# A two-layer hybrid backbone step: expert chunks in two halves over nine slots, single ada chunks, a two-expert first part

## The reference, cut to what matters

```python
def trunk_layer(x, mod, l, P, ctx):
    sh1, sc1, g1, sh2, sc2, g2 = split(mod)                # mod = silu(c) @ ada_w[l] + ada_b[l]
    h = rmsnorm(x, P['norm1_g']) * (1 + sc1) + sh1
    x = x + g1 * mixer_block(h)                            # attention, Mamba-2 scan, mLSTM, gated and merged
    h = rmsnorm(x, P['norm2_g']) * (1 + sc2) + sh2
    return x + g2 * expert_choice_ffn(h, ...)

def ssd_scan(...):                                         # per chunk of 128 tokens, both directions
    decay = exp(where(causal, seg, -inf))                  # seg = acum_i - acum_j
    y_diag = einsum('bcihn,bcjhn->bcijh', Cc, Bc) * decay * dt_j  @ xc

def expert_choice_ffn(h, router_w, w_gate, w_up, w_down):  # 16 experts; each takes its best tokens
    aff = softmax(xt @ router_w);  g, idx = top_k(aff.T, cap)        # cap = 16 context, 32 latent
    xe = xt[idx]
    hid = silu(xe @ w_gate) * (xe @ w_up)                  # 1024 x 1024 each
    out.at[idx].add((hid @ w_down) * g)
```

## Time and profile before

| | us |
|---|---|
| median of 3 runs (lowest, highest) | 2168.41 (2166.9, 2176.54) |
| the profiled execution's own time | 2157.21 |
| its span | 2155.4 |
| PE busy | 1932.9 (90%) |
| DVE busy | 632.4 (29%) |
| ACT busy | 419.7 (19%) |
| DMA | 546.5 MB, mean 254 GB/s |

### The profile page before, as it was taken

One profiled execution on the slowest core, in us unless ns is written; L12 is line 12 of the kernel. 1 busy time (PEld: TensorE's weight loads), 2 busy tenths in 40 slices (PEclk: granted clock), 3 DMA queues, 4 the chain that ended last, 5 costly groups with the idle time before them and its releaser, 6 DMA issues. The chain is left out here.

```text
span 2155.4 us, 21845 instructions
## 1 busy us (share of the span) xinstructions
PE 1932.9 (90%) x8320; PEld 1000.1 (46%) x8320; DVE 632.4 (29%) x1640; ACT 419.7 (19%) x957; POOL 38.4 (2%) x67
## 2 busy tenths in 40 slices
PE   6998989999988898988999899899988898989887
PEld 3554645555544433343354455554555334343433
DVE  1223335434241213121022242453443222131202
ACT  2122312222111111111121223212221111111112
POOL 0000000000000000000000000000000000000000
PEclk9999989999999999999999999999998999999999
DMA  8325242312698999999942422423145799999994
GB/s 348 109 78 195 86 161 98 108 55 87 245 359 373 427 398 427 428 427 428 415 169 72 175 97 85 184 95 121 41 178 212 282 429 422 429 427 427 428 428 189
DMA packets 81510, 546.52 MB, mean 254 GB/s; under 512 B 6976, under 2 KB 10048, under 8 KB 50560
## 3 DMA queue, kind: packets, MB, share of 16 engines
q1 hardware_dynamic: 79104, 536.76, 61.2%
q0 software_dynamic: 1872, 7.54, 0.9%
q10 hardware_dynamic: 432, 0.84, 0.1%
HBM read 541.44 MB, written 3.67 MB: 253 GB/s over the span
## 5 line engine op out<-in xcount | busy, mean ns | idle before, releaser
L827 PE MATMUL bank_D<-HM,ring 128*128 128x384 f32 x1600 | 553.3, 503 | 25.4 <-DVE AD L1677 6.4
L827 PEld LDWEIGHTS bank_D<-HM,ring 128*128 128x128 f32 x1600 | 308.1, 197 | 239.3 <-issue 49.8
L1272 PE MATMUL bank_D<-ring,HM 128*64 128x512 f32 x1024 | 238.6, 616 | 8.9 <-DVE HM L2177 8.9
L833 PE MATMUL bank_D<-ring,HM 128*128 128x512 f32 x384 | 169.0, 596 | 0.0
L1272 PEld LDWEIGHTS bank_D<-ring,HM 128*64 128x64 f32 x1024 | 87.1, 143 | 147.2 <-issue 136.8
L2186 DVE TENSOR_TENSOR EB<-EB,bank_D 128x512 f32<-128x512 f32 x32 | 22.0, 688 | 429.5 <-ACT EB L1609 429.5
L990 PE MATMUL bank_D<-YT,ring 128*128 128x384 f32 x384 | 125.9, 488 | 5.3 <-issue 3.2
L1296 PE MATMUL bank_Y<-ring,EB 128*64 128x512 f32 x512 | 115.2, 596 | 11.7 <-issue 11.7
L1272 PE MATMUL bank_D<-arena_a,HM 128*64 128x512 f32 x512 | 117.6, 601 | 6.3 <-DVE HM L2177 6.3
L833 PEld LDWEIGHTS bank_D<-ring,HM 128*128 128x128 f32 x384 | 71.8, 190 | 85.7 <-issue 84.4
L990 PEld LDWEIGHTS bank_D<-YT,ring 128*128 128x128 f32 x384 | 72.3, 190 | 54.6 <-issue 6.5
(11 more groups left out here) (279 smaller groups left out, 1781.0 us busy)
## 6 DMA issues: line engine op xcount, KB each, us to landing
ring<-ex_w_gate SPq DMA_DIRECT2D x48, 2048.0 KB, 15.8
ring<-ex_w_down SPq DMA_DIRECT2D x32, 2048.0 KB, 23.8
ring<-ada_w SPq DMA_DIRECT2D x23, 2048.0 KB, 8.7
ring<-w_in SPq DMA_DIRECT2D x16, 2048.0 KB, 8.7
arena_a<-ex_w_up SPq DMA_DIRECT2D x16, 2048.0 KB, 17.7
arena_a<-ex_w_gate SPq DMA_DIRECT2D x16, 2048.0 KB, 19.9
arena_b<-ex_w_up SPq DMA_DIRECT2D x16, 2048.0 KB, 22.0
ring<-ex_w_up SPq DMA_DIRECT2D x16, 2048.0 KB, 17.1
```

Source lines behind the costliest of these rows:

```text
L827: last = mm(u.t[:, 0:N], w[:, kt, c * P:(c + 1) * P], src[:, kt, :], start=kt == 0, stop=kt == KT - 1)
L833: last = mm(u.t[:, :], HT[:, kt, tile(t)], w[:, kt, 0:CH], start=kt == 0, stop=kt == KT - 1)
L1272: last = mm(u.t[64 * c:64 * c + 64, :], XE[:, h * 4 + k, j, :], w[:, k, c * 512:(c + 1) * 512], start=h == 0 and k == 0, stop=h == 1 and k ...
```

## The change

- `RING` is 9. The new slot 8 lies in a new arena, `arena_c`, over tiles that the mixer stage alone uses (YT, TMP, RS, ROWS, part of the constants); its first chunk waits for the layer's last merge. For layer 1, POOL loads rows and constants again.
- Each expert chunk is two DMAs of 1 MB; the second signals `slot_rest_in`. PE waits for it before the third of its four k-steps.
- `MIX_CHUNKS` has the ada chunks one at a time in other places, and `schedule` appends each ada step to a filler instead of making units of two.
- Group 0's first part holds experts 0 and 1; its ranks are done before the first gather, its second part is gathered after expert 1.
- `gather` a takes bank Y(a // 2) instead of Y(a % 2).
- The drain of `down` is split: ACT copies YES, DVE copies YEC and, after a wait for `latent_copied`, signals.
- The diagonal product: dt moves into the exponent (Ln of dt on ACT, subtracted on DVE), the two directions are added on DVE, and PE multiplies the sum with XS; XD is gone.
- The tail of a layer: `sum` two steps behind `scatter`, a table load moved ahead, TMP's part taken over by EB.

```diff
-RING = 8
+RING = 9
 MIX_CHUNKS = (
-    [("q", Q0), ("k", K0), ("v", V0), ("z", Z0), ("x0", X0), ("x1", X0 + CH)]
-    + [("ada", c) for c in range(4, 8)]
-    + [("gate", 0), ("gate", 1), ("branch", 0), ("branch", 1)]
-    + [("mq", MQ0), ("if", IF0 - 16), ("ada", 8), ("ada", 9), ("gate", 2), ("ada", 10), ("ada", 11), ("gate", 3), ("mv", MV0)]
-    + [("branch", 2), ("branch", 3), ("mo", MO0), ("gate", 4), ("gate", 5), ("branch", 4), ("branch", 5)]
+    [("q", Q0), ("k", K0), ("v", V0), ("z", Z0), ("ada", 4), ("x0", X0), ("ada", 5), ("x1", X0 + CH), ("ada", 6)]
+    + [("gate", 0), ("ada", 7), ("gate", 1), ("branch", 0), ("branch", 1)]
+    + [("mq", MQ0), ("ada", 8), ("if", IF0 - 16), ("gate", 2), ("ada", 9), ("gate", 3), ("ada", 10), ("mv", MV0)]
+    + [("branch", 2), ("branch", 3), ("mo", MO0), ("ada", 11), ("gate", 4), ("gate", 5), ("branch", 4), ("branch", 5)]
...
     dense = [[("z", t)] for t in range(TT)] + [[("x", j)] for j in range(6)] + [[("dt",)]]
+    dense[2] += [("ada", 4)]
+    dense[6] += [("ada", 5)]
+    dense[9] += [("ada", 6)]
+    dense += [[("gate", 0, d)] + {3: [("ada", 7)], 4: [("ada_turn", 1)]}.get(d, []) for d in range(KT)]
     fold = {"dt": ("dt_fold",), "if": ("if_fold",)}
-    dense += [[("ada", 4), ("ada", 5)], [("ada", 6), ("ada", 7)]]
-    dense += [([("ada_turn", 1)] if d == 1 else []) + [("gate", 0, d)] for d in range(KT)]
...
-                fillers.append([step for step in dense[0] if step[0] != "ada_turn"])
+                fillers.append([step for step in dense[0] if step[0] not in ("ada", "ada_turn")])
...
-    dense += [[("mq", j)] for j in range(4)] + [[("if",)], [("ada", 8), ("ada", 9)]]
-    for d in range(KT):
-        dense += [([("ada_turn", 2)] if d == 5 else []) + [("gate", 1, d)]] + ([[("ada", 10), ("ada", 11)]] if d == 3 else [])
+    dense += [[("mq", j)] + ([("ada", 8)] if j == 3 else []) for j in range(4)] + [[("if",)]]
+    dense += [[("gate", 1, d)] + {3: [("ada", 9)], 7: [("ada", 10)]}.get(d, []) for d in range(KT)]
...
-    s += ([("ada_next", 0)] if more else []) + [("softmax",), ("rank", 0)] + ([("ada_next", 1)] if more else [])
-    s += [("pick", 0), ("rank_spread", 1)] + ([("ada_sum", 0), ("ada_sum", 1)] if more else [])
+    s += ([("ada_next", 0)] if more else []) + [("softmax",), ("rank_spread", 0), ("rank_spread", 1)]
+    s += ([("ada_next", 1)] if more else []) + [("rank", 0), ("rank", 1), ("rank_spread", 2), ("pick", 0), ("rank_spread", 3)]
+    s += [("ada_sum", 0), ("ada_sum", 1)] if more else []
...
-        if g == 0 and j == 0:
+        if g == 0 and j == 1:
             s += [("gather", a, 1) for a in (0, 2, 1, 3)] + [("g_turn",)]
...
     if kind == "gather":
-        return [f"Y{step[1] % 2}"]
+        return [f"Y{step[1] // 2}"]
...
-    return (0, GE) if g else ((0, 1) if part == 0 else (1, GE))
+    return (0, GE) if g else ((0, 2) if part == 0 else (2, GE))
...
-        order = (3, 4, 5, 6, a, 7, b, c) if more else (3, 4, 5, 6, b, c, a, 7)
+        order = (3, 4, 5, 6, 8, a, 7, b, c) if more else (3, 4, 5, 6, 8, b, c, a, 7)
...
-                sp.dma_start(slot(at), src.rearrange("a e (p k) n -> p (a e k n)", p=P)).then_inc(slot_in[at], 16)
+                src = src.rearrange("a e (p k) n -> p (a e k n)", p=P)
+                n = KT * CH // 2
+                sp.dma_start(slot(at)[:, 0:n], src[:, 0:n]).then_inc(slot_in[at], 16)
+                sp.dma_start(slot(at)[:, n:2 * n], src[:, n:2 * n]).then_inc(slot_rest_in[at], 16)
...
+                elif at == 8 and key[0] == "expert" and key[1] < RING:
+                    sp.wait_ge(merged, l * 16 + 16)
...
+                    pool.dma_start(ROWS, A["rows"][one].to_broadcast([P, ROW_N])).then_inc(rows_in, 16)
+                    pool.dma_start(CT_MIX, A["constants"][:, FIRST_CONSTS:]).then_inc(more_consts_in[l], 16)
...
-                        for d in range(2):
-                            last = mm(u.t[:, head], EB[:, g, d, tile(h)], XD[:, d, head], start=d == 0, stop=d == 1)
+                        last = mm(u.t[:, head], EB[:, g, 0, tile(h)], XS[:, t, head], start=True, stop=True)
...
                     for k in range(4):
+                        if k == 2:
+                            wait_rest(l, g, j * 6 + h * 2 + x)
...
-                        copy(YES[rows, at], u.t[64 * c:64 * c + 32, :])
-                        last = copy(YEC[rows, at], u.t[64 * c + 32:64 * c + 64, :])
-                    last.then_inc(u.drained, 1)
+                        last = copy(YES[rows, c * 512:c * 512 + 512], u.t[64 * c:64 * c + 32, :])
+                    last.then_inc(latent_copied, 1)
...
+                elif kind == "down":
+                    for c in range(2):
+                        ve.tensor_copy(YEC[rows, c * 512:c * 512 + 512], u.t[64 * c + 32:64 * c + 64, :])
+                    fence()
+                    dve.wait_ge(latent_copied, l * EXPERTS + g * GE + j + 1)
+                    ve.tensor_copy(R3[:, 0:1], R3[:, 0:1]).then_inc(u.drained, 1)
...
-                    for d in range(2):
-                        dve.wait_ge(e_exp, l * 18 + ((t * 2 + g) * 2 + d + 1))
-                        e = EB[:, g, d, :].rearrange("p (h c) -> p h c", h=4)
-                        tt(e, e, CB[:, t, tile(g)].unsqueeze(1).to_broadcast([P, 4, P]), ALU.mult).then_inc(m_ready, 1)
+                    dve.wait_ge(e_exp, l * 18 + ((t * 2 + g) * 2 + 2))
+                    tt(EB[:, g, 0, :], EB[:, g, 0, :], EB[:, g, 1, :], ALU.add)
+                    fence()
+                    e = EB[:, g, 0, :].rearrange("p (h c) -> p h c", h=4)
+                    tt(e, e, CB[:, t, tile(g)].unsqueeze(1).to_broadcast([P, 4, P]), ALU.mult).then_inc(m_ready, 1)
```

More of the change, by code:

```diff
@@ L159, in schedule @@
         s += x
-    dense += [[("mo", t)] for t in range(TT)] + [[("gate", 2, d)] for d in range(KT)]
+    dense += [[("mo", t)] + ([("ada", 11)] if t == TT - 1 else []) for t in range(TT)]
+    dense += [[("gate", 2, d)] + ([("ada_turn", 2)] if d == 0 else []) for d in range(KT)]
     s += [("k_turn", t) for t in range(TT)]
@@ L247, in group_schedule @@
     for d in range(KT):
-        s += [("scatter", d)] + ([("sum", d - 1)] if d else []) + ([("ada_next", 3), ("ada_sum", 3)] if more and d == 4 else [])
-    return s + ([("ada_next_turn",)] if more else []) + [("sum", KT - 1)]
+        s += [("scatter", d)] + ([("sum", d - 2)] if d > 1 else []) + ([("ada_next", 3), ("ada_sum", 3)] if more and d == 5 else [])
+    return s + [("sum", KT - 2)] + ([("ada_next_turn",)] if more else []) + [("sum", KT - 1)]
 FLUSH = ("ada_turn", "y_turn", "merge", "k_turn", "cstate", "mo_sig", "out", "norm_sum", "norm_h")
@@ L262 @@
              "turn", "dt_fold", "if_fold", "stab", "acum", "y_turn", "z_sig", "mo_sig", "xs_turn", "b_turn", "x_turn"}
-DVE_STEPS = {"ada", "ada_turn", "ada_sum", "gather", "ada_next_turn", "norm_h", "rope", "v", "turn", "score", "att_y", "merge", "z_sig", "dt_fold", "conv", "acum", "state", "xd",
+DVE_STEPS = {"ada", "ada_turn", "ada_sum", "gather", "ada_next_turn", "norm_h", "rope", "v", "turn", "score", "att_y", "merge", "z_sig", "dt_fold", "conv", "acum", "state",
              "decay", "diag", "mb_y", "if_fold", "bcum", "urow", "cstate", "erow", "num", "ml_y", "out", "softmax", "rank", "next_rank", "pick", "next_pick",
@@ L283, in banks_of @@
         return [f"R{step[1] % 2}"]
-    if kind == "rank" and step[1]:
+    if kind == "rank":
         return []
@@ L490 @@
     HELD[_slot] = _before + [(_l, _key)]
+REST_AT = {(l, key): sum(k[0] == "expert" for _, k in held[:i + 1]) for held in HELD.values() for i, (l, key) in enumerate(held)}
 class Hardware:
@@ L706, in _ @@
                     sp.wait_ge(last.filled, last.after)
-                elif before is not None and at not in (4, 5, 6) or key[0] == "expert" and key[1] >= RING or key[0] == "ada" and l:
+                elif before is not None and at not in (4, 5, 6, 8) or key[0] == "expert" and key[1] >= RING or key[0] == "ada" and l:
                     chunk_free(*before)
@@ L1262, in group_step @@
                     if x == 0 and j in (0, experts_of(g, 1)[0]):
-                        for semaphore, value in drains([use(here, ("gather", a, min(j, 1))) for a in (h, 2 + h)]):
+                        for semaphore, value in drains([use(here, ("gather", a, int(j > 0))) for a in (h, 2 + h)]):
                             pe.wait_ge(semaphore, value)
@@ L2069, in mixer_step @@
                 elif kind == "rank":
-                    rank(use(here, step), 0)
+                    rank(use(here, ("rank_spread", step[1])), step[1])
                 elif kind == "pick":
-                    pick_one(0)
+                    pick_first(range(*experts_of(0, 0)))
                 elif kind == "softmax":
@@ L2161, in group_step @@
                 elif kind == "rank":
-                    rank(use(here if step[1] > 1 else Place(l), ("rank_spread", step[1])), step[1])
+                    rank(use(Place(l), ("rank_spread", step[1])), step[1])
```

141 lines of the change are left out of this document (78 added, 63 removed).

## The result

The changed kernel takes 2192.39 us (median of 4, 2188.14 to 2199.55), the kernel before 2167.68 (median of 4, 2166.9 to 2176.54): 1.0109 times as long, with a 95% interval of 1.0083 to 1.0134. It is slower by 1.1%. The forecast was slower by 0.5%, 2179: the direction is right, the size is under half.

What follows compares the result with a forecast made beforehand. PE was taken to bound the kernel, in the expert stage by a small margin over DMA. Savings of 46.6 less costs of 57.3 made 10.7 us slower than 2157.2: 2168, plus an 11.2 offset 2179; range 2140 to 2202.

Steps and rivals of the forecast that it cites:

- f: PE's granted clock: two more gaps of 6 us per layer, less the ones removed, cost 3 us.
- c: Attention stretches: single ada chunks make PE wait for held drains, 26.1 us of gaps against 9.1 before; 33.5 over both layers.
- a: Group 0 starts later, with more ranks and picks on DVE before the first gather: 3.1 us in all.
- b: Expert stage at the DMA edge: faster PE uses up the stream's lead, halves lose 0.5% rate; stalls of 4 us in all.
- Rival C: PE's clock falls after the new gaps, 300 us of mixer at 0.91 instead of 0.96: +15, 2194 us; chance 0.09.
- Gather banks: Expert groups 1 to 3: alternating banks remove 12 waits of 1.32 us for ACT's drain, 15.8 us saved.
- d: State and decay stretch: gaps around single ada steps, 16.6 us against 10.7 before; 11.1 us added over both layers.
- e: cstate.2 waits behind ada.11, 1.3 us in each of two layers: 2.6 us added.
- Down split: Expert groups: down drain shared by ACT and DVE cuts the scatter's wait from 2.52 to about 1.7; 6.4 us saved.
- Two-expert first part: Group 0: second gather takes 6.75 us instead of 11.2, first part's second pair saves 1.25; 11.5 us over two layers.
- Rival A: Held drains don't bite, ACT reaches them before PE needs the bank: 37 us comes off, 2142 us; chance 0.28.
- the tail: End of a layer: sum two steps behind and table load earlier save about 1 us each, 2 in all.

Runs made afterwards that it cites:

- e1: The changed kernel with the ada chunks back in pairs, in their old load order and places: 2120.36 us, 0.9783 of the kernel before.
- e4: The kernel before with the single ada chunks alone, load order and places as in the change: 2245.2 us, 1.0362 of the kernel before.
- e9: e5 with the gather banks as before the change, steps 0 and 2 sharing a bank: 2151.34 us, 0.9926 of the kernel before.
- e3: The changed kernel with each expert chunk as one transfer again, still nine slots: 2187.4 us, 1.0078 of the kernel before.
- e10: e5 with the drain of down by ScalarE alone, four copies: 2120.58 us, 0.9785 of the kernel before.
- e11: e5 with one expert in group 0's first part and three in the second: 2113.61 us, 0.9758 of the kernel before.
- e2: The changed kernel with the held drain done before each ada step, single ada chunks kept: 2139.45 us, 0.9876 of the kernel before.
- e5: The changed kernel with ada chunks in pairs and whole expert chunks, nine slots: 2112.02 us, 0.972 of the kernel before.
- e8: e1 with eight slots instead of nine: 2128.0 us, 0.9798 of the kernel before.
- e7: The changed kernel with the held drain done ahead of ada.5 alone: 2182.02 us, 1.0043 of the kernel before.

## Why the prediction was wrong

The direction was right, the size was not: 24.7 us by the medians for a forecast of 10.7 (2179 for 2192). The mechanism that it named is the one that the runs show; the step that failed is **f, the clock**, put at 3 us.

The runs split the miss. Terms c to f, the ada chunks with their clock, were put at 50.2 us; e1 takes them back and is 72 faster, e4 adds them to the kernel before and is 77 slower. All the rest was put at a gain of 39.5 (46.6 less a and b); e1 shows 48. So the cost is 22 us larger than forecast and the gain 8.5 larger. The sum treated a microsecond of PE's idle time as worth itself on both sides and left the clock to f; with the gather waits, whose removal was put at 15.8, e9 shows the same on the side of the gains.

- **c, the ada chunks: 26.1 us of gaps in attention forecast, 24.9 measured** (25.6 as length less busy time). The gap of 6.3 is 6.39, 1.95 is 2.0, 1.2 and 1.3 are 1.2 and 1.3, the 2.4s are 2.4 to 2.5; one transpose wait of 1.9 did not come. A written order of steps, with banks counted and durations from the trace, gave most of these gaps to a few tenths. Over both layers the added idle time in attention is 31.4 us for 33.5.
- **f, the clock: 3 forecast.** In attention alone the same matmuls are busy 11.0 us longer in layer 0 and 9.7 in layer 1. Over the whole kernel PE is busy 8.0 us longer although some 10.7 us of diagonal matmuls are gone: 19 net, after the expert stages gave 5.6 and 2.1 back. That is 16 of the 25 us by which the sum (10.7) missed the difference of the traces (35.8); the other 9 are idle time, 7.5 of them the waits for chunks (below). The clue was at hand: the stretch with the long gaps had 0.91, the group of experts 0.99. I read it and then priced two new gaps, not the twelve waits that I had just counted; 127 us of busy time at 0.91 for 0.99 would have been 11 us, twice over. Rival C named it and its 2194 lies next to the 2192 measured, but it had a chance of 0.09; and its 15 on top match in part by luck, since a cost 22 too small and a gain 8.5 too small come to 14.
- **Gather banks, 15.8 forecast:** the waits went as written; e9 puts the whole at 39 us with the clock (45 by ratios).
- **d and e:** the gaps 1.65, 3.3, 3.3, 5.75 came as 1.66, 3.51, 3.51 and 5.95, and e's 1.3 as a second wait at its line (3.5 us in two, for 2.2 in one). But the last one falls into the mLSTM stretch, which has also lost clock (0.92 in layer 1).
- **a:** in front of the first gather of layer 0, PE waits 0.38, 1.95 and 0.55 us where it had waited 0.81; with layer 1 it is 3.5 more, for the 3.1 that was put.
- **b, the DMA edge:** the chunks move at 421 GB/s for 428, 1.6%, where I had taken 0.5% of a range of 0 to 4. Waits of 0.55 per half at the end of the last group add up to 6.3 and 5.2 us, where I had 2 per layer. Whole chunks win 3.8 and 5.5 us of it (e3). The 341 GB/s that the Trainium skill, "DMA: Bandwidth & Descriptors" (Bandwidth), gives for a transfer of 1 MB did not come about: in a full queue the halves moved at 421, one every 2.49 us.
- **Down split:** 2.52 became 1.77, as forecast (about 1.7); e10 gives 9 us for it by medians and 14 by ratios for 6.4, not well separated from noise.
- **Two-expert first part, 11.5 forecast:** the second gather takes 6.2 us where 6.75 was forecast, and 11.2 before. With one expert and alternating banks it takes 8.2 (e11), so 3 of the 5 us do not need the second expert. The expert stages lose 8 us without the second expert; the total loses 2 or 8 (unclear).
- **Rival A** (drains reached in time) is refuted by the timeline and by e1, e2 and e4.
- **The offset** of 11.2 between the profiled execution and the median: it was that execution's, with a granted clock of 0.969, and it was not passed on. Other executions of the kernel before, beside the experiments, had 0.957 to 0.973 and 2153 to 2179 us; the profile of after lies at its own median. By medians the miss is 14 us (24.7 for 10.7), by traces 25. So part of the clock term in the traces is this one execution of before, not the change; e1, e2 and e4, timed in turns, are free of that.

Still open: the diagonal product, the tail and the table loads were not run by themselves; the trace gives 0.9 x 12 us for the first. The stretches behind the expert stages are 3.7 and 3.1 us shorter where the tail was put at 2 in all, but only 1 us of that is idle time; the rest is busy time at a higher clock (1.00 for 0.96 and 0.92 for 0.83). Why one and the same order of steps gets 0.93 in one execution and 0.96 in others (the scan of e5 and of e8 to e11) is not settled either.

## What to carry to other kernels

Where one pool of banks rotates through all steps and drains are held back, a step added singly shifts the parity of everything behind it: count the banks along the written order before moving a step. Price idle time of PE by what the granted clock does to the matmuls around it as well: here 16 us of idle time in a stretch came with 11 us of slower matmuls, and removing 16 us of small, regular waits saved 39 to 45. Judge bundles by their parts: this one held 48 us of gain and 72 us of loss, and the loss was a reordering beside the point of the rest.

## What the runs showed of the hardware

- The same 507 matmuls of attention were busy 127.0 us at a granted clock of 0.99 and 138.0 at 0.90, in stretches with 9.8 and 25.6 us of idle time. In the second the clock was 0.50 in five spells of some 3 to 10 us, each at a cluster of PE's waits.
- Taking away one wait of 6.39 us took away the spell around it and left the other four (e7).
- The same scan steps took 142.6 to 147.7 us in one execution each of six kernels (e1, e5, e8 to e11), at granted clocks of 0.93 to 0.96.
- 1984 expert matmuls were busy 404.7 us with 45.1 idle and 419.0 with 52.3 idle: ten more waits of 1.1 to 1.3 us in the layer came with it (e5, e9).
- Expert chunks moved as 1 MB transfers ran at 421 GB/s, as 2 MB transfers at 427 to 428, both with the queue full at a share of 1.01.
